# Later layers of a two-block transformer: each tile's result is worked on behind the next slot's first attention step, head norms start a slot earlier, and one group of output matmuls per head pair

## The reference

```
for l in range(2):
    h = rmsnorm(x, attn_norm[l]);  proj = h @ w_in[l]           # 1024 x 3072
    sb = stick_breaking(sb_q, sb_k, sb_v)       # 8 heads of 64, softplus and a running sum along keys
    attn = softmax(q0 k0) - lam * softmax(q1 k1)                # 4 differential heads, rope on q and k
    df = rmsnorm(attn @ v, subln_norm[l]) * (1 - lambda_init)   # the norm of a head
    x = x + concat(sb, df) @ w_o[l]
    h = rmsnorm(x, mlp_norm[l]);  x = x + relu(h @ w_ff1[l])**2 @ w_ff2[l]
return rmsnorm(x, final_norm)
```

## Time and profile before

| what | us |
|---|---|
| median of 3 runs | 1651.09 (1650.61 to 1651.24) |
| the profiled execution, its own time | 1651.25 |
| its span in the profile | 1649.4 |
| PE busy | 1570.8 (95%) |
| DVE, ACT, POOL busy | 922.3, 697.2, 230.3 |
| differential slots 5 to 17, layer 0 | 418.3 to 543.0 |
| stick-breaking slots 18 to 26, layer 0 | 543.0 to 639.7 |
| the same two stretches, layer 1 | 1048.4 to 1161.4 and 1161.4 to 1259.4 |

### The profile page before, as it was taken

The page is one execution under the profiler, slowest core; times in us unless marked ns, Lnnn a source line. Parts: engine busy times, 40 slices in busy tenths (PEclk is TensorE's granted clock), DMA queues, the critical chain, the costliest instruction groups (busy, mean ns, idle before and its releaser), DMA issues.

```text
span 1649.4 us, 21028 instructions
## 1 busy us (share of the span) xinstructions
PE 1570.8 (95%) x7937; PEld 1272.8 (77%) x7937; DVE 922.3 (56%) x1467; ACT 697.2 (42%) x1180; POOL 230.3 (14%) x167
## 2 busy tenths in 40 slices
PE   5998999999789899999999999989899999999998
PEld 4766888877667677888888888767677888888886
DVE  7666557576655786643434345655776543434343
ACT  4356542545353674432323234453574432323232
POOL 3000222022512222100000002122222100000001
PEclk8999999999999999999999999999999999999999
DMA  4201233322211112233323232221112233323331
GB/s 144 92 28 52 80 100 96 102 97 78 76 52 52 52 52 74 93 102 103 102 84 100 97 102 76 83 71 52 52 52 63 91 103 102 102 77 102 102 102 51
DMA packets 127270, 135.62 MB, mean 82 GB/s; under 512 B 2442, under 2 KB 120788, under 8 KB 127188
## 3 DMA queue, kind: packets, MB, share of 16 engines
q1 hardware_dynamic: 126084, 133.19, 24.7%
q0 software_dynamic: 288, 1.05, 0.2%
q10 hardware_dynamic: 816, 0.30, 0.1%
HBM read 132.43 MB, written 2.10 MB: 82 GB/s over the span
## 4 chain that ended last, share of the span: by engine, by line
PE 79%; DVE 12%; issue 4%; ACT 3%; DMA 1%; POOL 1%; SPq 0%; DVEq 0%; POOLq 0%; ACTq 0%
PE U L1405 22%; PE U L1407 22%; PE U L1406 22%; DVE W L1060 3%; PE U L1448 2%; PE U L1450 2%; PE U L1449 2%; DVE pr L938 1%; PE O L1647 1%; PE O L1631 1%; PE Z L1576 1%; PE Z L1591 1%; DVE pr L956 1%; DVE WL L888 1%; DMA raw<-in_attn_w_in 1%
## 5 line engine op out<-in xcount | busy, mean ns | idle before, releaser
L1405 PE MATMUL U<-XH,WL 128*128 128x512 f32 x976 | 386.9, 396 | 5.8 <-issue 5.1
L1407 PE MATMUL U<-XH,WH 128*128 128x512 f32 x976 | 381.4, 391 | 0.0
L1406 PE MATMUL U<-XL,WH 128*128 128x512 f32 x976 | 380.9, 390 | 0.0
L1405 PE MATMUL U<-MH,WL 128*128 128x512 f32 x848 | 339.0, 400 | 1.9 <-DVE tb L1280 1.7
L582 ACT ACTIVATE WH<-raw 128x1024 fp32r<-128x1024 f32 x246 | 257.4, 1050 | 191.7 <-PE U L1407 173.7
L1407 PE MATMUL U<-MH,WH 128*128 128x512 f32 x848 | 332.9, 393 | 0.0
L1406 PE MATMUL U<-ML,WH 128*128 128x512 f32 x848 | 332.7, 392 | 0.0
L888 DVE TENSOR_TENSOR WL<-raw,WH 128x1024 fp32r<-128x1024 f32 x210 | 269.7, 1284 | 64.9 <-ACT WH L582 54.2
L1405 PEld LDWEIGHTS U<-XH,WL 128*128 128x128 f32 x976 | 184.0, 188 | 45.4 <-issue 8.4
L1407 PEld LDWEIGHTS U<-XH,WH 128*128 128x128 f32 x976 | 183.8, 188 | 39.1
L1406 PEld LDWEIGHTS U<-XL,WH 128*128 128x128 f32 x976 | 184.2, 189 | 36.2
(11 more groups left out here) (211 smaller groups left out, 1759.5 us busy)
## 6 DMA issues: line engine op xcount, KB each, us to landing
raw<-in_w_ff SPq DMA_DIRECT2D x64, 1024.0 KB, 5.3
raw<-in_w_in SPq DMA_DIRECT2D x24, 1024.0 KB, 5.1
raw<-in_attn_w_in SPq DMA_DIRECT2D x10, 1024.0 KB, 5.2
raw<-in_pool_w_in SPq DMA_DIRECT2D x8, 1024.0 KB, 5.4
raw<-in_w_o SPq DMA_DIRECT2D x8, 1024.0 KB, 5.0
raw<-in_attn_w_out SPq DMA_DIRECT2D x4, 1024.0 KB, 5.0
raw<-in_pool_w_out SPq DMA_DIRECT2D x4, 1024.0 KB, 4.9
xin<-in_x SPq DMA_DIRECT2D x2, 1024.0 KB, 7.8
```

What stands on the lines that cost most here:

```text
L1405: mm(o, wl, xh, start=first, stop=False, **kw)
L1406: mm(o, wh, xl, start=False, stop=False, **kw)
L1407: return mm(o, wh, xh, start=False, stop=last, **kw)
```

## The change

DVE no longer takes a slot's result at the slot's end for slots 0 to 17: the next slot's list does it (`finish`), behind `df_evict` of part 1 and behind the first maximum step where there are any. The ACT copies for rope and the ACT part of the layer's statistics move in the same way (`shifted`), behind the eviction of the first turn. ACT does the first exponents ahead of `conv`. The head norm is listed in slot 7 + 3d, behind the output matmuls, where before it was in slot 8 + 3d. In the stick-breaking slots `conv` moves ahead of the last eviction on ACT, the second eviction moves ahead of the weights, and the output matmuls are one group at part 3.

More of the change, by code:

```diff
@@ L1129, in _ @@
+                for st in steps_of(s, "sb_o"):
+                    sb_low(st)
             df_mix = {l: {i + 1: st["d"] for i, x in enumerate(plan["layer", l]) for st in x["steps"] if st["op"] == "df_qk" and st["i"] == 2}
@@ L1331, in _ @@
-                    if kind == "dfk" and j == 0:
-                        dve.wait_ge(cs_landed, 16 * (l + 1))
-                    layer_slot(s, l, at, take, at not in POOL_LOW[l] and not s.get("second"))
-                    for i in range(s["n"]):
-                        take(i)
-                    for st in s["steps"]:
-                        if st["op"] == "stat":
-                            stat(st)
-                            if not st.get("res"):
-                                v.tensor_tensor(keys[:, 0, :], keys[:, 0, :], rstd[:, 0:S], ALU.mult)
-                                for i in range(2):
-                                    after(v.tensor_tensor(cs[:, i, :], cs[:, i, :], rstd[:, 0:S], ALU.mult))
+                    if s["kind"] == "dfk" and s["j"] == 0:
+                        dve.wait_ge(cs_landed, 16 * (l + 1))
```

95 lines of the change are left out of this document (49 added, 46 removed).

## The result

The changed kernel takes 1653.64 us (median of 20 runs, 1650.63 to 1657.01), the one before 1649.94 (20 runs, 1647.60 to 1651.72). The ratio is 1.0023 with a 95% interval of 1.0018 to 1.0029: it is slower by 3.7 us, where a gain of 1.2 was forecast. The profiled execution took 1655.35, with a span of 1653.6.

The account below looks back on a forecast made before the run. PE, busy 95% of the span, was taken as the bound. Layer 0 gains 1.6 - 0.4 = 1.2 us, layer 1 -0.9 + 0.9 = 0; with the median 0.2 below the profiled 1651.25, forecast 1650.0, range 1643 to 1656.

Parts of the forecast that it names:

- the waits only move: The forecast case: what is won at `df_f` is given back at later turns; a gain of 1.2 us, chance 0.46.
- S + 21.7: First turn of slot 10, layer 1, gets its operand 21.7 us after S, slot 8's start; PE waits about 7 us.
- The sums of slots 20, 22 and 24: Stick-breaking running sums on DVE wait for POOL's lock and take about 4.4 us instead of 2.3.
- The cycle from the second L1063 of a pair to that of the next: DVE-paced stick-breaking pairs, layer 1: slot 20 21.2 us (before 24.1), slot 22 22.4 and slot 24 22.9 (both before 21.2).
- The rival that the gain comes through: Rope in slot 9 and the sums escape POOL's lock: 4.6 us more a layer, or 1641; chance 0.29.
- its opposite: Sums fall behind POOL on both slots of each stick-breaking pair, cycle 23 us: 6 us worse, 1656; chance 0.25.
- slot 10 behind the turn: From slot 10's turn to rope's end some 6.0 us, where PE needs 4.2; a loss of 0.8 in layer 0.
- the half clock after the new wait: Slower matmuls behind slot 10's new wait: may cost 0 (hidden behind rope) to 1.7 us.
- slot 17: New PE wait, as DVE takes slot 16's second result only after head 3's norm: 0.9 us lost in each layer.
- layer 0 up to S: Slot 8 of layer 0 starts 3.5 us earlier: 3.7 wait and 1.6 of slower matmuls gone, combining 2.3 later.
- Slots 11 to 16: Differential slots after slot 10: a gain of 0.2 us in layer 0 and 0 in layer 1.
- Stick-breaking slots: Slots 18 to 26: layer 0 loses 0.4 us and layer 1 gains 0.9.

Follow-up runs that it names:

- experiment 3: The changed kernel with 27 idle matmuls on PE ahead of slot 10's first turn, overwritten by that turn: 1653.03 us, ratio 1.0020.
- e12: e9 with the 27 idle matmuls of experiment 3 ahead of slot 10's first turn: 1642.73 us (5 runs), ratio 0.9960.
- experiment 4: The changed kernel with DVE taking the second result of slot 16 ahead of the head norm: 1650.15 us, ratio 1.0000.
- experiment 1: The changed kernel with its stick-breaking part undone, differential slots as changed: 1651.08 us, ratio 1.0009.
- experiment 7: The changed kernel with `conv` behind the second softplus, not the first, in slots 18, 20, 22 and 24: 1647.19 us, ratio 0.9979.
- e11: The kernel before with the stick-breaking slots of e9, differential slots left as before: 1642.67 us (5 runs), ratio 0.9953.
- e9: The changed kernel with the edits of experiment 4 and experiment 7 together: 1648.01 us, ratio 0.9985.

## Why the prediction was wrong

The forecast had the sign wrong: -1.2 us where +3.7 was measured. Its range of 1643 to 1656 holds the time, and its likeliest range of 1647 to 1654 too.

**Right: the waits only move.** `df_f` waits for nothing; the turn of slot 10 is at S + 21.8 with a wait of 6.93, forecast S + 21.7 and about 7. The second maximum and rope's third operation meet POOL where it was said. The sums of slots 20, 22 and 24 take 4.4. Slot 7's gain in layer 1 is 1.9. The cycle from the second L1063 of a pair to that of the next, which is how the forecast counts it, is 20.8, 21.9 and 22.7 us in layer 1 (1185.42 and 1206.23 the first two), forecast 21.2, 22.4 and 22.9: each a little high, the order right. The rival that the gain comes through did not occur, nor did its opposite, that both sums of each pair meet the lock at 23 us a cycle. The time lies on the side of that last rival, but it got there through slots 10 and 17.

**The step that failed: slot 10 behind the turn.** The prediction says that the eviction and rope take "some 6.0 us from the turn to the end of rope, where PE needs 4.2", and that the half clock after the new wait may cost nothing, "hidden behind rope". The 6.0 is right at full clock: experiment 3 has 5.91. But the half clock is not hidden behind rope, because rope is itself behind PE. DVE's list has the eviction of the second turn ahead of rope, and PE reaches that turn 3.48 us after the first at half clock (1100.41 against 1096.93), 1.93 at full clock (1097.82 against 1095.89 in e3). The chain is turn, a part of v at PE's clock, second turn, DVE's eviction, rope, next part. So 7.24 instead of 5.91, 1.3 us in each layer, with slot 10 at 12.5 us, and at full clock (experiment 3) it takes 11.2, near the 11.3 and 11.0 of the forecast. So what was mis-sized is the half clock, put at nothing. I had written the upper bound of 1.7 beside it and taken the lower one. Filling the wait gave back 1.1 and 1.3 us in the profile of both experiments 3 and 12, and a faster median in 12.

**Mis-sized: slot 17.** 0.9 was forecast for each layer, 1.3 measured. In layer 1 slot 17 starts at 1160.00. DVE's norm ends at 1163.38, 3.4 us in where I had 3.2, a handover of 0.2 that I had left out follows, and PE goes on at 1164.14, 4.1 us in against 3.8. Taking the result ahead of the norm removes the wait (experiment 4).

**Mis-sized: layer 0 up to S.** -3.5 forecast, -3.0 over all profiles, -1.6 in this pair, by the scatter of slot 5. The terms that the prediction names, 3.7 and 1.6 won and 2.3 lost, add up to 3.0 and not to 3.5; no run shows the other 0.5. Slots 11 to 16 went the other way, 0.6 us shorter in each layer where 0.2 and 0 were forecast.

**Stick-breaking slots.** +0.9 and -1.6 against +0.4 and -0.9. Against the more usual 96.6 of layer 1 (experiment 1) the order gains nothing, so the -0.9 rested on one execution of before in which slot 20 had more half-clock matmuls. The term is a small part of the error. Experiment 7 shows a larger point beside it: the sums behind POOL, which I had netted against the earlier turns to a loss of 0.4 us in layer 0, cost 3.9 and 2.8 us in the two layers against an order in which `conv` stands behind the second softplus.

**What stays open.** The profile's terms explain 3.7 us of one pair of executions; the halves of the change measured separately, +1.0 and +0.3 us, add to less, within their intervals. What the wait in slot 17 is worth in the median is between 0 and 3.5 us, and the half clock between 0.6 and 5.3; the profile says 2.7 and 2.4. Why e11 beats e9 by 5.3 us is answered in part. In the two profiles the differential slots 5 to 17 take the same, 232.8 us in both layers together against 233.2; the stick-breaking slots, with the same order in both, take 3.8 us less, all of it in slot 20 (12.24 and 13.80 against 14.95 and 15.01). What differs in every execution is the mean granted clock: 0.991 to 0.994 in the five of e11, 0.990 to 0.992 in the five of e12, 0.981 to 0.985 in the eleven of e9. So e9 spends more of its time at half clock, and not only in slot 10; why slot 20 stays in it longer behind the same wait of 3.0 us is open.

## What to carry to other kernels

When several waits of one engine are fed by one chain on others, moving a wait out of the way does not shorten it: add up the chain from its start (here maxima, exponents, shift, rope, combining), and if its end does not move, expect the waits to come back in one piece. One long wait can be worse than two short ones (here slot 10 took 12.5 us behind 6.9, and 11.2 behind 3.3 and 1.5), since half clock behind it may fall where nothing hides it; and before that half clock is called hidden behind a step, ask whether the step waits for TensorE. Where two engines lock each other out, the cheapest move is often to issue the long operation on the side engine one step later: here that one line was worth 6.5 and 7.8 us in two pairs of kernels, more than any other edit. And a list of waits is no measure of a stretch: with that line the turns waited 4.7 us longer in all while the stretch got 3.9 and 2.8 us shorter.

## What the hardware showed that I had not expected

**The clock after a wait.** After a wait of 6.93 us in a stretch that is otherwise full, the granted clock is 0.50 for 5 us and the matmuls are 0.22 us apart instead of 0.12. With the wait filled it stays at 1.00; the window of e3 from the turn on:

```profile
1095.80:1099.80 4.00, 3.91 (x33) 3.91 (x34) 1.98 (x6) 2.95 (x5) 0.00 (x0) 1.00 0.70 244
```

The Trainium skill (TensorE: Matmul & The Clock Gate, HAM oscillation — how this bites in real kernels) has the same for a loop that waits for DMA in every tile: the next tile starts at half rate. The window of the changed kernel agrees (0.50 behind the wait); here the wait is for a chain on two other engines.

**Scatter of the clock.** The same order of the same slots gives different half-clock stretches from profile to profile: layer 0's slot 5 took 10.50 to 11.89 us, slot 20 in the order of experiment 7 took 12.24 to 15.01. The waits in front of them agree to 0.1 us. Behind the 3.4 us wait in slot 9 of layer 1 the granted clock of slots 8 and 9 was 0.92 before and 1.00 in e11. A term of 1 us read from one execution is uncertain by as much as that where half clock is in it.

**Who is not blocked.** Rope's third operation, `queries`' last one with two inputs in SBUF, was held while POOL ran from 1092.76 to 1095.17. But in slot 8 two custom maxima L985, which read `Z`, ran inside POOL's operation of 1082.90 to 1085.30 in 0.28 us each (128 columns, at 1083.09 and 1083.30), as they do at 1115.80 and 1116.01 with POOL idle. Only L990, on 128 x 4 numbers in SBUF, took 1.69 in slot 8, and 0.17 at 1116.33.
